# A fused transformer layer's expert stage: 192-row visits run four chunks of split products, then the raw products of the same four

## The chip, the cores and the metric

The kernel runs on one core of one Trainium2 chip. Its time is the time of one execution in microseconds; the median of several is given, and one more execution is profiled.

## The reference

One layer over 1024 latent tokens and 256 context tokens of width 1024, all float32: modulated RMSNorm, attention and a bidirectional mLSTM side by side, an output projection, and then a routed feed-forward with 32 experts, of which each token takes 4. The change touches the last part alone:

```python
def expert_block(args):
    xb, e = args
    gu = xb @ w_gu[e] + b_gu[e]
    glu = jnp.minimum(gu[:, :D_FF], SWIGLU_LIMIT)
    lin = jnp.clip(gu[:, D_FF:], -SWIGLU_LIMIT, SWIGLU_LIMIT)
    return (glu * jax.nn.sigmoid(SWIGLU_ALPHA * glu) * (lin + 1)) @ w_down[e] + b_down[e]
```

Here `w_gu[e]` is 1024 x 2048 and `w_down[e]` 1024 x 1024. The result of each row, times its gate and the modulation, is added to the token's row.

## The kernel before

The kernel is seven phases; the last, `phase_experts`, takes from about 905 us to the end. It goes over the experts in **visits**. A visit takes one expert and some of its rows; the experts are ordered by how many rows they have, and a visit's kind gives how many rows it takes. `MIXED` takes 192: a full part of 128 rows and a raw part of 64. `FULL` takes 128, `WIDE` 256 (two full parts), `NARROW` 64 and `LEAST` 32 (raw parts alone), `SPILL` 128. The order is six pairs of MIXED and FULL, two of MIXED and NARROW, three of WIDE and LEAST, three of WIDE and NARROW, then the spill visits. So there are eight MIXED visits.

**Weights.** An expert's weights are 12 chunks of 128 x 2048 (1 MB each), chunks 0 to 7 of `w_gu`, 8 to 11 of `w_down`, in 12 buffers `w[c]`. SP loads chunk c of the next visit when chunk c of this one is done with: for a visit behind a MIXED one when `s_used` has counted it (L2143, L2152), for the one behind a FULL visit when `s_lo` has (L2147). Chunks 0 to 3 make the first half of gate and up, 4 to 7 the second, 8 to 11 the result.

**Two kinds of product.** A full part uses split products. ACT copies a chunk to a high part `wh` (rounded, L2458, `s_hi`), DVE subtracts to get the low part `wl` (L2575, `s_lo`); there are three slots of each (`SLOTS`), chunk c has slot c % 3. PE multiplies high rows by high, high by low, low by high: 3 matmuls for each of 2 halves and 2 k-steps, 12 of 128 x 128 by 512 columns a chunk (L2312 for gate and up, L2326 for the result). A raw part uses the float32 chunk itself with a stationary operand of 64 columns, two column tiles side by side (L2307, L2321); the profile counts 8 such instructions a chunk.

**PE's order in a MIXED visit** (`visit` of the tensor block): for each chunk both parts, the full one first for even c, the raw one first for odd c. So raw products of two chunks stand together: full 0, raw 0, raw 1, full 1, full 2, raw 2, raw 3, full 3, and so on. The bias of the full part (L2297) opens the visit, that of the raw part (L2293) stands ahead of raw 0; both second ones stand ahead of chunk 4. Behind chunk 5 PE turns the first half of the hidden rows (L2283, six transposes), behind chunk 8 the second half, behind chunk 9 and behind chunk 10 the next visit's rows (L2272, four each); those behind chunks 8 and 10 thus stand between two raw products. `s_used` is raised once a chunk, by its last matmul.

**ACT** writes the high part of chunk c when `s_used` says that chunk c - 3 is done with (`split`, `this`, `ahead` for the next visit's first three), and between them the silus (L2470) and the high parts of turned rows. **DVE** writes the low parts, and when `s_used` says that four chunks are done it clamps gate and linear of both parts (`clamped`, L2593, L2598), multiplies them (`hidden`, L2607, `s_h`), takes the low parts of turned rows (L2568) and at the end the result (`result`, L2638, L2635). Each engine's order is written out by hand and is strict: what stands behind a wait waits with it. **POOL** gathers the rows of the visit after the next when PE has turned the next one's (`s_tp`) and scatters results.

Of the kernel before, what the change touches and what calls it, by code (L numbers as in the profile page):

```python
# [12 lines left out]
ALU = mybir.AluOpType  # L13
# [2036 lines left out]
def phase_experts(nc, a, m, PS):  # L2050
# [6 lines left out]
    with semaphores(nc, "experts") as sem:  # L2057
# [78 lines left out]
        with nc.Block() as block:  # L2136
# [127 lines left out]
            def _(pe):  # L2264
# [119 lines left out]
                with pe.Fori(0, N192) as i:  # L2384
                    visit(2 * i, 2 * i, MIXED, FOR_SMALL, 48 * i + 16)
                    visit(2 * i + 1, 2 * i + 1, FULL, FOR_BIG, 48 * i + 48)
                with pe.Fori(N192, NWIDE0) as i:
                    visit(2 * i, i + N192, MIXED, FOR_SMALL, 48 * i + 16)
                    visit(2 * i + 1, None, NARROW, FOR_BIG, 48 * i + 48)
# [40 lines left out]
            def _(act):  # L2430
# [47 lines left out]

                def visit(v, parts, before, following, banks, next_split, last=False):

                    def this(c):
                        split(c, v, v * NW + (c - SLOTS + 1))

                    def ahead(c):
                        if next_split:
# [32 lines left out]
                with act.Fori(0, N192) as i:  # L2518
                    visit(2 * i, MIXED, 6 * i, FULL, FOR_SMALL, True)
                    visit(2 * i + 1, FULL, 6 * i + 4, MIXED, FOR_BIG, True)  # L2520
                for i in range(N192, NWIDE0):
                    visit(2 * i, MIXED, 6 * i, None, None, False)
                    narrow(2 * i + 1, NARROW, 6 * i + 4, MIXED if i + 1 < NWIDE0 else WIDE)
# [33 lines left out]
            def _(dve):  # L2557
# [27 lines left out]

                def clamped(parts, j, v, before):

                    dve.wait_ge(s_used, v * NW + (4 * j + 4))
                    first = before + len(parts) * j
                    for p, part in enumerate(parts):  # L2590
                        b = part.second if j else part.first
                        n = H // part.tiles if part.tiles else H
                        dve.tensor_scalar(hid[p][:, 0:n], PS[:, b[0], 0:n], 7.0, ALPHA, ALU.min, ALU.mult).then_inc(s_g, 1)  # L2593
                    for p, part in enumerate(parts):
                        b = part.second if j else part.first
                        n = H // part.tiles if part.tiles else H
                        up = PS[:, b[0], n:2 * n] if part.tiles else PS[:, b[1], :]
                        dve.tensor_scalar(lin[p][:, 0:n], up, 7.0, -7.0, ALU.min, ALU.max).then_inc(s_cd, 1)  # L2598

# [41 lines left out]

                def visit(v, col, parts, before, n_split, n_eh, following, banks, next_split, last=False):

# [9 lines left out]
                    this(5)  # L2653
                    clamped(parts, 0, v, before)
                    this(6)
# [4 lines left out]
                    this(9)  # L2660
                    clamped(parts, 1, v, before)
                    hidden(parts, 1, before)
# [20 lines left out]
                def narrow(v, parts, col, before, n_split, n_eh, following=WIDE):  # L2683

                    tiles = parts[0].tiles

                    def keep_hidden(half, bank):
                        dve.wait_ge(s_tp, 4 * v + (3 + (2 * half if parts is LEAST else half)))
                        dve.tensor_scalar(hTr[0][:, 4 * half:4 * half + 4, 0:P // tiles], folded(bank, tiles), 1.0 / ALPHA, None, ALU.mult).then_inc(s_el, 1)
                    clamped(parts, 0, v, before)  # L2690
# [4 lines left out]
                    clamped(parts, 1, v, before)  # L2695
                    hidden(parts, 1, before)
                    keep_hidden(1, parts[0].upper)
                    split(0, n_split * NW + 1)
                    turn_kept(xT, 0, following, FOR_BIG[0], n_eh)
                    split(1, n_split * NW + 2)  # L2700
                    turn_kept(xT, 1, following, FOR_BIG[1], n_eh + 2)
                    result(parts, v)
                    split(2, n_split * NW + 3)
                with dve.Fori(0, N192) as i:
                    visit(2 * i, 3 * i, MIXED, 6 * i, 2 * i, 12 * i + 4, FULL, FOR_SMALL, True)
                    visit(2 * i + 1, 3 * i + 2, FULL, 6 * i + 4, 2 * i + 1, 12 * i + 10, MIXED, FOR_BIG, True)
                for i in range(N192, NWIDE0):
                    eh = 8 * i + 4 * N192
                    visit(2 * i, 3 * i, MIXED, 6 * i, i + N192, eh + 4, None, FOR_SMALL, False)
                    narrow(2 * i + 1, NARROW, 3 * i + 2, 6 * i + 4, i + (N192 + 1), eh + 8, MIXED if i + 1 < NWIDE0 else WIDE)  # L2710
# [142 lines left out]
```

## Time and profile before

| | |
|---|---|
| median of 3 runs | 2443.32 us (2442.1 to 2449.93) |
| the profiled execution | 2440.65 us, its span 2438.8 us |
| PE busy | 2330.0 us, 96% of the span |
| DVE, ACT busy | 1575.3 and 1078.0 us |
| mean granted TensorE clock | 0.979 of full speed |
| DMA | 556.74 MB, 228 GB/s over the span |

PE is TensorE's matmuls, PEld its weight loads, DVE VectorE, ACT ScalarE, POOL GpSimd, SP the engine that issues the loads. In a timeline, matmuls of one kind that follow one another are merged into one row with their count; a matmul's own duration is longer than the distance to the next, because they are pipelined, so runs are measured from start to start.

### The profile page before, as it was taken

How to read it: one execution, taken by the hardware profiler on the slowest of the kernel's cores; microseconds unless marked ns; L12 is line 12 of the kernel's file. 1: busy time of each engine (PE TensorE's matmuls, PEld its weight loads, DVE VectorE, ACT ScalarE, POOL GpSimd, SP SyncE). 2: the span in 40 equal slices, each digit the busy share in tenths (PEclk: the TensorE clock that was granted, in tenths of full speed). 3: DMA queues.
4: the chain of work that ended last, by engine and by line, in shares of the span. 5: the costliest groups of instructions: out<-in, count | busy, mean ns of one | idle time of the engine just before them, and what ended most of it. 6: DMA issues, size and time to landing. Idle time of an engine off the chain costs nothing.

```text
span 2438.8 us, 34440 instructions
## 1 busy us (share of the span) xinstructions
PE 2330.0 (96%) x12022; PEld 1612.1 (66%) x12022; DVE 1575.3 (65%) x1911; ACT 1078.0 (44%) x1392; POOL 526.1 (22%) x487
## 2 busy tenths in 40 slices
PE   5999988999998959999999999999999999999997
PEld 3997674555556746676766766557778768667775
DVE  3332756767656676876877867455556555549998
ACT  3332333444454234564655655324333323327776
POOL 0000041555676021111211211101100110102112
PEclk8999999999999969999999999999999999999999
DMA  8450031000013376987978979889789988979997
GB/s 300 156 179 23 19 106 75 8 4 7 1 55 106 123 260 221 326 281 265 338 252 295 322 248 316 295 315 367 270 302 379 318 299 306 332 247 386 382 386 259
DMA packets 241305, 556.74 MB, mean 228 GB/s; under 512 B 27841, under 2 KB 32354, under 8 KB 240098
## 3 DMA queue, kind: packets, MB, share of 16 engines
q1 hardware_dynamic: 225680, 509.49, 58.5%
q0 software_dynamic: 12704, 45.75, 7.0%
q8 instruction: 52, 0.85, 0.1%
q10 hardware_dynamic: 2834, 0.36, 0.1%
q14 instruction: 35, 0.29, 0.0%
HBM read 520.18 MB, written 34.96 MB: 228 GB/s over the span
## 4 chain that ended last, share of the span: by engine, by line
PE 57%; DMA 1%; DVE 1%; issue 1%; ACT 1%; POOL 1%; DVEq 0%; ACTq 0%; POOLq 0%
PE PS L2312 28%; PE PS L2326 13%; PE PS L2307 8%; PE PS L2321 4%; DMA acc_dram<-y,idxs 1%; PE PS L2272 1%; PE PS L2283 1%; PE PS L2297 1%; ACT wh L2458 1%; DVE wl L2575 0%; PE PS L2293 0%; POOL rt L2259 0%; DVE y L2638 0%; DVE hid L2593 0%; DVE hTl L2568 0%
## 5 line engine op out<-in xcount | busy, mean ns | idle before, releaser
L2575 DVE TENSOR_TENSOR wl<-w,wh 128x2048 fp32r<-128x2048 f32 x312 | 713.3, 2289 | 232.9 <-ACT wh L2458 231.7
L2458 ACT ACTIVATE wh<-w 128x2048 fp32r<-128x2048 f32 x312 | 597.7, 1916 | 393.5 <-PE PS L2312 265.1
L2312 PE MATMUL PS<-wh,xTh 128*128 128x512 f32 x1024 | 333.2, 407 | 0.0
L2312 PE MATMUL PS<-wl,xTh 128*128 128x512 f32 x1024 | 316.5, 390 | 0.0
L2312 PE MATMUL PS<-wh,xTl 128*128 128x512 f32 x1024 | 315.8, 390 | 0.0
L2204 POOL COPY idxg<-tokens 128x1 int32 (+1 forms) x47 | 28.5, 624 | 1023.9 <-PE PS L2272 950.6
L2312 PEld LDWEIGHTS PS<-wh,xTh 128*128 128x128 f32 x1024 | 187.9, 189 | 66.3 <-issue 28.1
L2312 PEld LDWEIGHTS PS<-wl,xTh 128*128 128x128 f32 x1024 | 192.5, 188 | 41.5
L2312 PEld LDWEIGHTS PS<-wh,xTl 128*128 128x128 f32 x1024 | 192.5, 188 | 40.9
L2307 PE MATMUL PS<-w,xTr 128*64 128x512 f32 (+1 forms) x1216 | 210.1, 527 | 0.0
L1118 POOL TENSOR_TENSOR acc<-acc,probT 128x512 f32<-128x512 f32 x128 | 174.2, 1361 | 24.8 <-ACT probT L1176 12.0
L2326 PE MATMUL PS<-wh,hTh 128*128 128x512 f32 x512 | 165.7, 405 | 2.3 <-DVE hTl L2568 2.3
L2326 PE MATMUL PS<-wl,hTh 128*128 128x512 f32 x512 | 158.9, 391 | 0.0
L2326 PE MATMUL PS<-wh,hTl 128*128 128x512 f32 x512 | 158.2, 390 | 0.0
L2219 POOL DMA_INDIRECT acc_dram<-y,idxs x47 | 109.1, 2322 | 188.7 <-DVE y L2638 121.4
L2470 ACT ACTIVATE hid<-hid 128x512 f32<-128x512 f32 (+2 forms) x96 | 49.5, 543 | 215.9 <-DVE hid L2593 215.9
L2307 PEld LDWEIGHTS PS<-w,xTr 128*64 128x64 f32 (+1 forms) x1216 | 67.4, 128 | 113.2 <-issue 103.4
L1248 DVE TENSOR_REDUCE negmax<-PS 128x1 f32<-128x1280 f32 x64 | 95.5, 1492 | 56.4 <-PE PS L1377 55.7
L1176 ACT ACTIVATE probT<-PS 128x512 f32<-128x512 f32 x160 | 93.0, 597 | 87.7 <-PE PS L1399 81.2
L2326 PEld LDWEIGHTS PS<-wh,hTh 128*128 128x128 f32 x512 | 90.2, 188 | 32.0 <-issue 13.0
L2321 PE MATMUL PS<-w,hTr 128*64 128x512 f32 (+1 forms) x608 | 110.9, 532 | 0.0
L2326 PEld LDWEIGHTS PS<-wh,hTl 128*128 128x128 f32 x512 | 96.1, 188 | 21.3
(443 smaller groups left out, 3474.7 us busy)
## 6 DMA issues: line engine op xcount, KB each, us to landing
w<-in_w_gu_dram SPq DMA_DIRECT2D x544, 512.0 KB, 11.3
w<-in_w_down_dram SPq DMA_DIRECT2D x136, 1024.0 KB, 12.5
later_wmod<-in_w_mod_dram SPq DMA_DIRECT2D x8, 2048.0 KB, 8.0
wmod<-in_w_mod_dram SPq DMA_DIRECT2D x8, 1024.0 KB, 14.5
x<-in_x_dram SPq DMA_DIRECT2D x8, 512.0 KB, 7.8
rowm<-rowm_dram SPq DMA_DIRECT2D x16, 256.0 KB, 3.3
w_out<-in_w_out_dram SPq DMA_DIRECT2D x1, 4096.0 KB, 12.6
ox<-in_x_dram SPq DMA_DIRECT2D x8, 512.0 KB, 4.3
```

The lines of the kernel that those rows point to most:

```text
L1118: pool.tensor_tensor(acc[half][:, :], acc[half][:, :], probT[:, op + 1, :], ALU.add).then_inc(s_acc, 1)
L1176: act.activation(probT[:, n % NT, :], PS[:, T0 + n % 3, :], ACT.Exp).then_inc(s_ex, 1)
L1248: dve.tensor_reduce(negmax[:, u:u + 1], flat[:, 0:KEYS], AX.X, ALU.max, negate=True).then_inc(s_mx, 1)
L2204: pool.tensor_copy(idxg[p][:, :], m.tokens[:, bass.ds(col + p, 1)]).then_inc(s_pc, 1)
L2219: pool.indirect_dma_start(out=a["acc"], out_offset=bass.IndirectOffsetOnAxis(ap=idxs[p][0:n, 0:1], axis=0), in_=y[p][0:n, :], in_offset=No ...
L2307: mm = pe.matmul(PS[tile_rows(part, u), b[0], 0:2 * n], xTr[part.n][:, k, 0:P // part.tiles], wrv[c][:, kk, :, n * u:n * u + n], start=Fal ...
L2312: mm = pe.matmul(PS[:, b[g], :], x[part.n][:, k, :], ws[s][:, kk, g, :], start=False, stop=end and x is xTl)
L2321: mm = pe.matmul(PS[tile_rows(part, u), b[0], 0:D // part.tiles], hTr[part.n][:, k, 0:P // part.tiles], wdn[c][:, kk, tile_cols(part, u)], ...
L2326: mm = pe.matmul(PS[:, b[g], :], x[part.n][:, k, :], ws[s][:, kk, g, :], start=begin and x is hTh and ws is whv, stop=end and x is hTl)
L2458: act.activation(wh[c % SLOTS][:, :], w[c][:, :], ACT.Copy).then_inc(s_hi, 1)
L2470: act.activation(hid[p][:, 0:n], hid[p][:, 0:n], ACT.Silu).then_inc(s_sg, 1)
L2575: dve.tensor_tensor(wl[c % SLOTS][:, :], w[c][:, :], wh[c % SLOTS][:, :].bitcast(F32), ALU.subtract).then_inc(s_lo, 1)
```

## The change

A MIXED visit on PE gets a function of its own, `mixed`. In each of three quarters it runs the split products of four chunks and then the raw products of the same four. Each split chunk raises a new semaphore, `s_parts`; `s_used` is raised by the raw product of each chunk. All transposes now stand behind split products; the raw part's biases stand at the beginning of the raw run. ACT's high parts of MIXED visits, and the next visit's first three behind one, wait for `s_parts` in place of `s_used`. DVE clamps the full part on `s_parts` and the raw part on `s_used`, one behind the other. The helpers `gate_clamped` and `linear_clamped` are the old bodies of `clamped`.

```diff
+        s_parts = sem("chunk_parts_used_by_mixed")
...
+                def mixed(v, i, split, rows_in):
+                    full, raw = MIXED
+                    pe.wait_ge(s_sel, v + 1)
+                    for quarter in range(3):
+                        chunks = range(4 * quarter, 4 * quarter + 4)
+                        product = down if quarter == 2 else gate_up
+                        if quarter == 0:
+                            pe.wait_ge(s_el, 4 * v + 1)
+                            bias(full, 0)
+                        for c in chunks:
+                            pe.wait_ge(s_lo, split * NW + (c + 1))
+                            if c == 4:
+                                pe.wait_ge(s_y, v + 1)
+                                bias(full, 1)
+                            if c == 8:
+                                pe.wait_ge(s_el, 4 * v + 3)
+                            if c == 10:
+                                pe.wait_ge(s_el, 4 * v + 4)
+                            for kk in range(2):
+                                mm = product(full, c, kk)
+                            mm.then_inc(s_parts, 1)
+                            if c == 5:
+                                pe.wait_ge(s_h, 2 * v + 1)
+                                turn_hidden(MIXED, 0)
+                            if c == 8:
+                                pe.wait_ge(s_h, 2 * v + 2)
+                                turn_hidden(MIXED, 1)
+                            if c == 9:
+                                pe.wait_ge(s_xg, rows_in)
+                                turn_rows(FOR_SMALL, 0)
+                            if c == 10:
+                                turn_rows(FOR_SMALL, 1)
+                        if quarter == 0:
+                            pe.wait_ge(s_el, 4 * v + 2)
+                            bias(raw, 0)
+                        if quarter == 1:
+                            bias(raw, 1).then_inc(s_bias, 1)
+                        for c in chunks:
+                            for kk in range(2):
+                                mm = product(raw, c, kk)
+                            mm.then_inc(s_used, 1)
...
-                    visit(2 * i, 2 * i, MIXED, FOR_SMALL, 48 * i + 16)
+                    mixed(2 * i, i, 2 * i, 48 * i + 16)
...
-                def split(c, v, used):
+                def split(c, v, used, by=s_used):
...
-                        act.wait_ge(s_used, used)
+                        act.wait_ge(by, used)
...
+                        if parts is MIXED:
+                            split(c, v, nth * NW + (c - SLOTS + 1), s_parts)
...
+                        if next_split and parts is MIXED:
+                            split(c, v + 1, nth * NW + (NW + c - SLOTS + 1), s_parts)
...
+                    if parts is MIXED:
+                        dve.wait_ge(s_parts, nth * NW + (4 * j + 4))
+                        gate_clamped(0, parts[0], j)
+                        linear_clamped(0, parts[0], j)
+                        dve.wait_ge(s_used, v * NW + (4 * j + 4))
+                        gate_clamped(1, parts[1], j)
+                        linear_clamped(1, parts[1], j)
+                        return
```

## Rows read from the trace of the kernel before

**Rows 1.** The page: PE's busy time, and DVE's costliest group

```profile
PE 2330.0 (96%) x12022; PEld 1612.1 (66%) x12022; DVE 1575.3 (65%) x1911; ACT 1078.0 (44%) x1392; POOL 526.1 (22%) x487
...
L2575 DVE TENSOR_TENSOR wl<-w,wh 128x2048 fp32r<-128x2048 f32 x312 | 713.3, 2289 | 232.9 <-ACT wh L2458 231.7
```

**Rows 2.** PE's longest waits, 905 to 2390 us: us, times, longest one

```profile
PE PS L2297 <- DVE xTl L2568: 6.3, 5, 2.2
```

**Rows 3.** By stretch: length, busy PE, PEld, DVE, ACT, POOL; clock, DMA share, GB/s

```profile
1006.70:1066.70 60.00, 60.00 (x270) 35.14 (x269) 39.83 (x34) 27.21 (x23) 8.67 (x7) 1.00 0.75 254
1066.70:1103.20 36.50, 36.50 (x173) 29.65 (x172) 33.97 (x27) 26.56 (x20) 7.75 (x7) 1.00 1.00 351
...
1549.50:1573.80 24.30, 24.30 (x122) 8.80 (x122) 11.11 (x17) 7.09 (x9) 4.72 (x3) 1.00 1.02 334
```

**Rows 4.** Timeline of PE, one MIXED visit: start, us, instructions

```profile
1006.68 0.61 PE L2297 MATMUL PS<-bias,sel 96*128 96x512 bf16 x2
...
1009.96 0.41 PE L2293 MATMUL PS<-bias,sel 96*64 96x512 bf16 x2
...
1013.73 0.73 PE L2312 MATMUL PS<-wh,xTh 128*128 128x512 f32 x2
...
1016.59 0.62 PE L2312 MATMUL PS<-wh,xTh 128*128 128x512 f32 x2
...
1019.40 3.65 PE L2307 MATMUL PS<-w,xTr 128*64 128x512 f32 x16
1022.98 0.73 PE L2312 MATMUL PS<-wh,xTh 128*128 128x512 f32 x2
...
1025.84 0.61 PE L2297 MATMUL PS<-bias,sel 96*128 96x512 bf16 x2
...
1026.71 0.73 PE L2312 MATMUL PS<-wh,xTh 128*128 128x512 f32 x2
...
1036.09 0.82 PE L2283 MATMUL PS<-ident,hid 128*128 128x128 f32 x6
...
1039.57 3.65 PE L2307 MATMUL PS<-w,xTr 128*64 128x512 f32 x16
...
1048.82 1.94 PE L2321 MATMUL PS<-w,hTr 128*64 128x512 f32 x8
1050.69 0.88 PE L2283 MATMUL PS<-ident,hid 128*128 128x128 f32 x6
...
1053.36 0.73 PE L2326 MATMUL PS<-wh,hTh 128*128 128x512 f32 x2
...
1066.69 0.61 PE L2297 MATMUL PS<-bias,sel 96*128 96x512 bf16 x2
```

**Rows 5.** Timeline of PE, in a FULL and in a NARROW visit

```profile
1067.60 0.62 PE L2312 MATMUL PS<-wl,xTh 128*128 128x512 f32 x2
...
1072.59 0.61 PE L2312 MATMUL PS<-wh,xTh 128*128 128x512 f32 x2
...
1549.77 7.04 PE L2307 MATMUL PS<-w,xTr 128*64 128x512 f32 x32
1556.63 0.38 PE L2293 MATMUL PS<-bias,sel 96*64 96x512 bf16 x2
...
1573.77 0.61 PE L2297 MATMUL PS<-bias,sel 96*128 96x512 bf16 x2
...
1574.69 0.62 PE L2312 MATMUL PS<-wl,xTh 128*128 128x512 f32 x2
```

**Rows 6.** Timeline of DVE, second half of MIXED, then first of NARROW

```profile
1046.21 1.02 DVE L2593 TENSOR_SCALAR hid<-PS 128x512 f32<-128x512 f32 x2 [0.41 <-PE PS L2312]
...
1048.74 1.03 DVE L2607 SCALAR_TENSOR_TENSOR hid<-lin,hid 128x512 f32<-128x512 f32 x2 [0.58 <-ACT hid L2470]
...
1556.85 0.43 DVE L2593 TENSOR_SCALAR hid<-PS 128x256 f32<-128x256 f32 x1 [4.51 <-PE PS L2307]
...
1557.84 0.43 DVE L2607 SCALAR_TENSOR_TENSOR hid<-lin,hid 128x256 f32<-128x256 f32 x1 [0.23 <-ACT hid L2470]
```

More of the change, by code:

```diff
@@ L2384, in _ @@
                 with pe.Fori(0, N192) as i:
-                    visit(2 * i, 2 * i, MIXED, FOR_SMALL, 48 * i + 16)
+                    mixed(2 * i, i, 2 * i, 48 * i + 16)
                     visit(2 * i + 1, 2 * i + 1, FULL, FOR_BIG, 48 * i + 48)
                 with pe.Fori(N192, NWIDE0) as i:
-                    visit(2 * i, i + N192, MIXED, FOR_SMALL, 48 * i + 16)
+                    mixed(2 * i, i, i + N192, 48 * i + 16)
                     visit(2 * i + 1, None, NARROW, FOR_BIG, 48 * i + 48)
@@ L2477, in bias_parts, with visit @@
                     act.activation(gparts[:, :, :], graw[:, :, :], ACT.Copy).then_inc(s_gk, 1)
-                def visit(v, parts, before, following, banks, next_split, last=False):
+                def visit(v, parts, before, following, banks, next_split, last=False, nth=None):
                     def this(c):
-                        split(c, v, v * NW + (c - SLOTS + 1))
+                        if parts is MIXED:
+                            split(c, v, nth * NW + (c - SLOTS + 1), s_parts)
+                        else:
+                            split(c, v, v * NW + (c - SLOTS + 1))
                     def ahead(c):
-                        if next_split:
+                        if next_split and parts is MIXED:
+                            split(c, v + 1, nth * NW + (NW + c - SLOTS + 1), s_parts)
+                        elif next_split:
                             split(c, v + 1, v * NW + (NW + c - SLOTS + 1))
@@ L2584, in _, with gate_clamped, linear_clamped, clamped @@
                 dve.wait_ge(s_gb, 16)
-                def clamped(parts, j, v, before):
+                def gate_clamped(p, part, j):
+                    n = H // part.tiles if part.tiles else H
+                    bank = (part.second if j else part.first)[0]
+                    dve.tensor_scalar(hid[p][:, 0:n], PS[:, bank, 0:n], 7.0, ALPHA, ALU.min, ALU.mult).then_inc(s_g, 1)
+                def linear_clamped(p, part, j):
+                    b = part.second if j else part.first
+                    n = H // part.tiles if part.tiles else H
+                    up = PS[:, b[0], n:2 * n] if part.tiles else PS[:, b[1], :]
+                    dve.tensor_scalar(lin[p][:, 0:n], up, 7.0, -7.0, ALU.min, ALU.max).then_inc(s_cd, 1)
+                def clamped(parts, j, v, before, nth):
+                    if parts is MIXED:
[6 more added lines that the diff above has]
+                        return
                     dve.wait_ge(s_used, v * NW + (4 * j + 4))
-                    first = before + len(parts) * j
                     for p, part in enumerate(parts):
-                        b = part.second if j else part.first
-                        n = H // part.tiles if part.tiles else H
-                        dve.tensor_scalar(hid[p][:, 0:n], PS[:, b[0], 0:n], 7.0, ALPHA, ALU.min, ALU.mult).then_inc(s_g, 1)
+                        gate_clamped(p, part, j)
                     for p, part in enumerate(parts):
[L2595 to L2598, printed above, removed]
+                        linear_clamped(p, part, j)
                 def hidden(parts, j, before):
@@ L2640, in result, with visit @@
                     ins.then_inc(s_y, 1)
-                def visit(v, col, parts, before, n_split, n_eh, following, banks, next_split, last=False):
+                def visit(v, col, parts, before, n_split, n_eh, following, banks, next_split, last=False, nth=None):
                     def this(c):
@@ L2653, in visit @@
                     this(5)
-                    clamped(parts, 0, v, before)
+                    clamped(parts, 0, v, before, nth)
                     this(6)
@@ L2660, in visit @@
                     this(9)
-                    clamped(parts, 1, v, before)
+                    clamped(parts, 1, v, before, nth)
                     hidden(parts, 1, before)
@@ L2689, in keep_hidden @@
                         dve.tensor_scalar(hTr[0][:, 4 * half:4 * half + 4, 0:P // tiles], folded(bank, tiles), 1.0 / ALPHA, None, ALU.mult).then_inc(s_el, 1)
-                    clamped(parts, 0, v, before)
+                    clamped(parts, 0, v, before, None)
                     hidden(parts, 0, before)
@@ L2694, in narrow @@
                     keep_hidden(0, parts[0].lower)
-                    clamped(parts, 1, v, before)
+                    clamped(parts, 1, v, before, None)
                     hidden(parts, 1, before)
@@ L2704, in _ @@
                 with dve.Fori(0, N192) as i:
-                    visit(2 * i, 3 * i, MIXED, 6 * i, 2 * i, 12 * i + 4, FULL, FOR_SMALL, True)
+                    visit(2 * i, 3 * i, MIXED, 6 * i, 2 * i, 12 * i + 4, FULL, FOR_SMALL, True, nth=i)
                     visit(2 * i + 1, 3 * i + 2, FULL, 6 * i + 4, 2 * i + 1, 12 * i + 10, MIXED, FOR_BIG, True)
```

6 lines of the change are left out of this document (3 added, 3 removed).

## The prediction

> **What bounds the kernel now.** The page first: PE is busy for 2330.0 of the 2438.8 us span [rows 1]. What matters is the expert stage, from 905 to 2390 us, and there the longest entry in the list of PE's waits is 6.3 us, in five waits [rows 2]. The busy time by stretch shows a 192-row visit and the 128-row visit behind it: PE is busy for all 60.00 and all 36.50 us, at a granted clock of 1.00, that is at 2.4 GHz; DVE has 39.83 and 33.97 us of work in them [rows 3]. So PE sets the time in every mixed visit, and only what shortens PE's own stream, or makes it wait, can move the end. The timeline of PE shows one such visit as runs of split products (L2312, L2326) and of raw products (L2307, L2321); it lasts from 1006.68 to 1066.69, 60.01 us [rows 4]. There are 8 of them (6 before full visits, 2 before narrow ones).
>
> **No product is removed.** Two pitches come from runs without a turn in them. Split matmuls: from 1067.60 to 1072.59 eleven pairs start, 4.99 us, 0.2268 each, so a chunk of 12 takes 2.72 us [rows 5]. Raw: the narrow visit's 32 matmuls, four chunks, start at 1549.77 and the next thing at 1556.63, so a chunk takes 1.715 us [rows 5]. A mixed visit needs 12 of each: 32.7 + 20.6 = 53.2 us. The other 6.8 us are biases, transposes and turns between the two kinds of run, and of these the change takes a part.
>
> **Turns.** From 1013.73 to 1022.98 PE does two split chunks and two raw ones and is back at the same point: 9.25 us for 2 x 2.72 + 2 x 1.715 = 8.87 us [rows 4]. A turn there and back costs 0.38 us. Its parts: the first split chunk takes 2.86 us (entry 0.14), the second 2.81 (leaving 0.09), the raw pair 3.58 instead of 3.43 (0.15). Before, the raw chunks go in pairs (0 with 1, 2 with 3, and so on), six raw runs a visit; after, there are three runs of four chunks. Three turns fewer: 3 x 0.38 = 1.14 us.
>
> **Transposes that leave the raw run.** The six hidden transposes behind chunk 8 stand inside a raw pair: from 1048.82 to 1053.36 is 4.54 us, against 3.58 for a raw pair alone, so they cost 0.96. The same six behind chunk 5 stand between split chunks: from 1036.09 to 1039.57 they and a split chunk take 3.48 us, less 2.81 for the chunk: 0.67 [rows 4]. After the change all stand between split chunks: 0.29 us less. The four row transposes behind chunk 10 move in the same way; what goes is the second entry and leaving of a raw run around them, not their own time, so I cost them the same, 0.29 (bounds 0 and 0.29).
>
> **Biases.** At chunk 4 the full part's bias and the raw part's bias stand between two split chunks: 1025.84 to 1026.71, 0.87 us, and an entry of 0.14: 1.01. After, the full bias stands ahead of a split run, which costs 0.47 (1006.68 to 1009.96 is 3.28, less 2.72 and 0.09), and the raw bias stands at a turn, which costs 0.19 (1009.96 to 1013.73 is 3.77, against 3.58) [rows 4]. That is 0.35 us less. And two of the three remaining returns to split work begin with a bias (chunk 4, the next visit's chunk 0): the bias then takes the place of the first split matmul, and the entry of 0.14 is gone, twice, 0.28 us. The trace shows raw, bias, split at the end of a narrow visit: from the bias at 1573.77 to the third split matmul at 1574.69 is 0.92 us, and behind split products, from 1066.69 to 1067.60, it is 0.91 [rows 4, 5]. A raw run of four chunks between two split runs is not in the trace; I price it by the pitch of 1.715 and one entry and leaving.
>
> **The sum.** 1.14 + 0.29 + 0.29 + 0.35 + 0.28 = 2.35 us a visit, and 8 visits give 18.8 us. Without the row transposes' 0.29 it would be 2.06 and 16.5 us. The profiled execution takes 2440.65 us, so it would take 2421.9; it lies 2.7 us under the median of the runs, 2443.32, and the forecast for the median is 2424.5 us.
>
> **Where something could come late.** Three things are rearranged for it.
> Hidden halves: DVE now clamps the full part when the split run ends, far ahead, and the raw part when the raw run ends. What PE then has before the hidden transposes is two split chunks and a bias at chunk 5 (0.26 + 5.7 us) and only chunk 8 at the second half (2.72 + 0.14 = 2.86 us, where before it was 1046.21 less 0.2 to 1050.69, 4.7 us). The path at the second half, priced from the narrow visit: raw run ends, DVE starts 0.22 later, and the raw product of gate and linear is done at 1558.27, 1.42 after 1556.85, with the silu within it [rows 5, 6]. The full part's product goes in ahead of the raw one: a pair takes 1.03 and the narrow one 0.43, so 0.6 more. The half is ready 0.22 + 1.42 + 0.6 = 2.2 us after the raw run, at the most, against 2.86: 0.6 us to spare. At chunk 5 a low part of 2.29 us (L2575 [rows 1]) lies in between: 4.5 against about 6.0. Queued behind DVE's new wait are the products, the gate columns, the selector and the low parts of chunks 6 and 10; the tightest of these, chunk 10, has chunk 9 and two groups of transposes of cover more than the half has. ACT's silu of the raw part waits for the same clamp.
> High and low parts: slots of the high part come free at the split product, and in a run of four split chunks ACT and DVE must deliver one per 2.72 us. The 128-row visit has just this pace, and PE is busy for 36.50 of 36.50 us in it [rows 3]. In the raw runs nothing is asked for, so they catch up; the added wait of ACT costs nothing there.
> Weight loads: SP issues the load of chunk c for the next visit when the raw product of c is done. Chunk 0's raw product now stands behind four split chunks instead of one, so its load goes out 8 us later, and that of chunk 8 some 11 us later (its raw run of two ended 16.0 us before the visit's end, at 1050.69; now it is done 5.2 before); SP stands behind each, the later loads with it. POOL's next gather, which waits for the row transposes, starts some 7 us earlier, out of the way of the last four loads. By the DMA's rate under (c) these loads have landed some 7 us into the visit behind, which asks for its chunk 8 over 14 us after its start, so I cost it at nothing. If loads were late, every microsecond would be PE's.
>
> The added signals are 12 increments a visit at the ends of split chunks. In the 128-row visit each chunk ends with one as well, and the 0.2268 pitch runs on through it [rows 5], so their price is nothing. The Trainium skill, page "TensorE: Matmul & The Clock Gate", section "The cost: per-tile semaphore tail", puts 26.3 ns on each increment; as an estimate from that page 96 of them would be 2.5 us and the time 2427.0. The trace speaks against it here, because the pitch has no room for it.
>
> **Rivals.** (a) The hidden half comes late. The whole path took 3.56 us before (1046.21 to 1049.77 [rows 6], with a high part in ACT's way); if it stays so long behind the raw run, PE waits 3.56 + 0.2 - 2.86 = 0.9 us a visit, 7.2 in all, and the time is 2431.7. For it: the margin is thin. Against: most of that path is the full part's, which is now done earlier. (b) The change doesn't do what it says: the 0.38 us goes with the chunks and not with the turns, as a loss that each raw chunk pays once its rows and weights alternate with split ones, and longer runs pay it all the same. Then nothing is gained: 2443. Against: the narrow visit's run of 32 shows no such loss. The Trainium skill, page "TensorEngine Tiling (Array Packing)", section "Key Properties", says that a change of tiling mode drains TensorE, which would be a price for each turn; it names no size, so the sum has none of it, and it is one reason why (b) has no more than 0.07. (c) Slower: the weights. In the last 5.2 us of a mixed visit four loads of 1.05 MB are freed, and the full visit's twelve follow; with gathers and scatters (an estimate: 320 rows of 4 KB in, as many out and added, some 3 MB) that is 19.8 MB. At the 351 GB/s of that stage [rows 3] they are in after 56 us, 15 us into the next mixed visit, with chunk 3 some 24 us earlier in the queue. PE asks for chunk 3 8.4 us into it, and the high and the low part need some 4.2 of them (2.29 for the low one [rows 1], somewhat less for the high one), so it must land by 4.2. It lands 9 us before the visit begins. If the bunched loads ran slower, chunk 3 would be late below 250 GB/s; at 210 GB/s it would be 8 us late in each of 8 visits, 64 - 19 = 45 us slower, 2488, and from about 230 down it is slower by what can be measured. For it: the DMA share is 1.00 in the full visit and 1.02 in the narrow one, and loads that were spread over the mixed visit now come in three bunches. Against: 351 and 334 GB/s were moved at just that share [rows 3]. In the two narrow pairs the margin is smaller (chunk 0 must land 20 us after the mixed visit's end, 24.3 less 4.2, and 8.2 MB, itself and some 3 MB of rows among them, have 25 us, 328 GB/s), but two visits a few microseconds late take back a part of the gain only; the range has them. (d) The clock: raw runs of 7 us might lower it. The narrow visit is nothing but raw runs, and the granted clock is 1.00 in it [rows 3], so I give this no chance.
>
> **How the numbers follow.** Forecast 0.81, (a) 0.08, (b) 0.07, (c) 0.04. Under 0.3% (7.3 us) two measurements of this kernel can't be told apart. Forecast and (a) are faster by more: 0.89; (b) is the same: 0.07; (c) is slower: 0.04. The range takes in the forecast with its bounds (savings of 16 to 19 us, and 3 us of difference between medians) and (a): 2420 to 2433.
>
> **What would show it.** In the profile after, a mixed visit lasts 57.7 us (57.5 to 58.2), with runs of 48, 24, 24 and three times 12 split matmuls and three runs of 32 raw ones; the raw runs take about 7.0 us each. The full and narrow visits keep 36.5 and 24.3 us, the wide ones stay as they are. PE's waits stay as short as they are; a new row of PE waiting for DVE's hidden product would be (a), PE or ACT waiting for a landing (c). The prediction is wrong if the visits keep 60 us with PE busy, or if PE idles ahead of chunk 3, chunk 9 or the hidden transposes.

## The result, and the profile after

| | before | after |
|---|---|---|
| median | 2444.82 us of 6 runs (2442.1 to 2451.38) | 2429.95 us of 6 runs (2425.31 to 2432.9) |
| ratio | | 0.9935, 95% interval 0.9924 to 0.9947 |
| profiled execution, its span | 2440.65, 2438.8 us | 2429.25, 2427.4 us |
| the 8 mixed visits, sum | 481.78 us | 463.98 us |
| of these, the five between two full visits, each | 60.01 us | 57.84 to 57.91 us |
| a full visit, a narrow visit | 36.5, 24.25 us | 36.5, 24.23 us |
| the three pairs of WIDE and LEAST and the three of WIDE and NARROW, sum | 537.35 us | 544.82 us |

The kernel became faster by 14.9 us in the medians (15.9 by the ratio, 13 to 19 by its interval), against 18.8 forecast; 2429.95 lies in the range of 2420 to 2433. The profiled executions differ by 11.4 us only, and the stretches say why: the mixed visits give 17.8 us, the pairs with wide visits, which the diff doesn't touch, take 7.5 back, all of it in the three wide visits behind LEAST ones. Of the 1.1 us that are left, 0.7 lie ahead of the first mixed visit (908.61 us before, 907.87 after).

One run below was a slow one, 3929.9 us at a granted clock of 0.556: one of the twelve of before with the rows moved, whose figures here leave it out.

The page of after, engines first. PE's busy time fell by 14.2 us, its idle time rose by 2.8 (108.8 to 111.6):

```profile
span 2427.4 us, 34446 instructions
PE 2315.8 (95%) x12022; PEld 1620.4 (67%) x12022; DVE 1571.3 (65%) x1911; ACT 1082.2 (45%) x1392; POOL 533.0 (22%) x487
```

The timeline of PE in one mixed visit of after (start, us, instructions), the one that answers to [rows 4]:

```profile
1003.63 0.60 PE L2298 MATMUL PS<-bias,sel 96*128 96x512 bf16 x2
...
1009.54 0.74 PE L2313 MATMUL PS<-wh,xTh 128*128 128x512 f32 x2
1010.12 0.63 PE L2313 MATMUL PS<-wl,xTh 128*128 128x512 f32 x2
...
1015.24 0.41 PE L2294 MATMUL PS<-bias,sel 96*64 96x512 bf16 x2
1015.48 7.03 PE L2308 MATMUL PS<-w,xTr 128*64 128x512 f32 x32
1022.45 0.60 PE L2298 MATMUL PS<-bias,sel 96*128 96x512 bf16 x2
...
1034.80 7.03 PE L2308 MATMUL PS<-w,xTr 128*64 128x512 f32 x32
1041.76 0.73 PE L2327 MATMUL PS<-wh,hTh 128*128 128x512 f32 x2
...
1044.62 0.82 PE L2284 MATMUL PS<-ident,hid 128*128 128x128 f32 x6
...
1054.52 7.09 PE L2322 MATMUL PS<-w,hTr 128*64 128x512 f32 x32
1061.54 0.61 PE L2298 MATMUL PS<-bias,sel 96*128 96x512 bf16 x2
```

Three raw runs of 32 matmuls, each 6.96 to 7.02 us from start to start, stand where six of 16 were; from the first bias to the last it is 57.91 us. The windows of that visit, of the full one behind it and of a narrow one answer to [rows 3] (length, then busy PE, PEld, DVE, ACT, POOL, granted clock, DMA share, GB/s):

```profile
1003.60:1061.50 57.90, 57.90 (x269) 35.84 (x268) 39.37 (x34) 29.68 (x24) 11.29 (x9) 1.00 0.71 250
1061.50:1098.10 36.60, 36.60 (x175) 29.70 (x174) 33.86 (x26) 24.66 (x19) 6.61 (x4) 1.00 1.04 371
1533.40:1557.60 24.20, 24.20 (x122) 8.85 (x118) 11.06 (x17) 7.17 (x9) 4.69 (x3) 1.00 1.03 355
```

PE is still busy all of the time, at 2.4 GHz, long raw runs included, and the bunched loads move at 371 and 355 GB/s. What changed elsewhere is in the list of PE's waits (us, times, longest one), which answers to [rows 2]:

```profile
PE PS L2298 <- DVE xTl L2617: 10.6, 7, 2.5
PE PS L2327 <- DVE hTl L2617: 1.6, 5, 0.3
```

The first line is a bias that waits for DVE's low part of turned rows: 10.6 us against 6.3. One of the seven waits opens the first visit, 2.2 us before and 2.1 after; the others stand at wide visits behind LEAST ones, three of them, 1.05 us each, ahead of the visit in both kernels. So two questions stand: are the 2.35 us a visit made of the steps that were summed, and do the 7.5 us in the wide visits come from the change?

### The profile page after: what moved, and what is told of

Read it like the earlier page. It is cut to its first block, busy times and chain, and to the rows that moved or that the text cites. A ratio compares the mean times of both kernels' runs of the same rounds, so it can differ in the third digit from the quotient of the medians.

```text
span 2427.4 us, 34446 instructions
## 1 busy us (share of the span) xinstructions
PE 2315.8 (95%) x12022; PEld 1620.4 (67%) x12022; DVE 1571.3 (65%) x1911; ACT 1082.2 (45%) x1392; POOL 533.0 (22%) x487
## 4 chain that ended last, share of the span: by engine, by line
PE 57%; DVE 2%; DMA 2%; issue 1%; ACT 1%; POOL 0%; DVEq 0%; ACTq 0%; POOLq 0%
PE PS L2313 28%; PE PS L2327 13%; PE PS L2308 7%; PE PS L2322 4%; DMA acc_dram<-y,idxs 2%; PE PS L2273 1%; PE PS L2284 1%; PE PS L2298 1%; ACT wh L2502 1%; DVE wl L2624 0%; PE PS L2294 0%; DVE y L2700 0%; DVE outs L2815 0%; DVE xTl L2617 0%; DVE rows L2811 0%
## 5 line engine op out<-in xcount | busy, mean ns | idle before, releaser
L2205 POOL COPY idxg<-tokens 128x1 int32 (+1 forms) x47 | 36.3, 790 | 971.7 <-PE PS L2273 897.8
L2638 DVE TENSOR_SCALAR hid<-PS 128x512 f32<-128x512 f32 (+2 forms) x96 | 55.6, 590 | 120.9 <-PE PS L2308 106.2
L2327 PEld LDWEIGHTS PS<-wl,hTh 128*128 128x128 f32 x512 | 96.1, 188 | 21.1
## 6 DMA issues: line engine op xcount, KB each, us to landing
wmod<-in_w_mod_dram SPq DMA_DIRECT2D x8, 1024.0 KB, 14.2
```

The costliest lines, as they stand in the source:

```text
L2327: mm = pe.matmul(PS[:, b[g], :], x[part.n][:, k, :], ws[s][:, kk, g, :], start=begin and x is hTh and ws is whv, stop=end and x is hTl)
L2638: dve.tensor_scalar(hid[p][:, 0:n], PS[:, bank, 0:n], 7.0, ALPHA, ALU.min, ALU.mult).then_inc(s_g, 1)
```

## Experiments on the mixed visit

**The same kernel once more,** to see which stretches repeat.

> The changed kernel once more, unchanged. In its profiled execution the eight 192-row visits took 57.6 to 57.9 us each (the first 59.24) against 60.0 to 60.1 before, 17.9 us less in all with the visits between them, but the three wide visits behind a 32-row visit took 73.60, 71.17 and 74.22 us against 71.12, 70.21 and 70.21, 7.5 us more. Theory A (chance): these three waits on landing weights, and the falls of the granted clock behind two of them, come and go between executions of either kernel; then the 192-row visits repeat to 0.1 us here and the three wide visits come out differently, and the ratio to before is 0.992 to 0.994. Theory B (caused by the change): the three wide visits take 71 to 74 us again, 4 us or more above before's in sum, and the gain stays at 11 to 16 us.

Measured: median 2428.54 us of 6 runs, ratio 0.9931 (0.9915 to 0.9947). The mixed visits sum to 464.07 us, 0.09 from the first profile. The three wide visits behind LEAST ones took 77.19, 73.93 and 70.19 us, against 73.60, 71.17 and 74.22 in the first profile of the same program. A mixed visit's length belongs to the kernel; that of a wide visit behind a LEAST one to the execution.

**Groups of two and of one.** PE's `mixed` with its chunks in groups of two (six raw runs, as before the change) or of one (twelve), transposes and biases where the change has them.

```diff
-                    for quarter in range(3):
-                        chunks = range(4 * quarter, 4 * quarter + 4)
-                        product = down if quarter == 2 else gate_up
+                    for group in range(NW // 2):
+                        chunks = range(2 * group, 2 * group + 2)
+                        product = down if chunks[0] >= 8 else gate_up
```

> Groups of two chunks in place of four: split 0, 1, raw 0, 1, split 2, 3, raw 2, 3 and so on, all else as in the changed kernel, so six raw runs a visit as before the change, but the transposes stand between split products and the biases at the turns. Theory of turns (0.38 us for a raw run's entry and leaving): a 192-row visit takes 57.85 + 3 x 0.38 = 59.0 us, somewhat less where the short split runs take away the wait at chunk 2 (some 0.1). Rival, the price goes with the chunks: 57.85 us, since no chunk is added or removed. A second rival, that all of the gain is the transposes and biases: 57.85 too.

> Groups of one chunk: twelve raw runs a visit. If each raw run costs 0.38 us, nine more than in the changed kernel: 57.85 + 3.4 = 61.3 us a visit, 1.2 us slower than before the change, and as 6 more turns than with groups of two 2.3 us above that kernel's visit. If the price goes with the chunks: 57.85. Whole kernel by the turns: some 27 us slower than the changed kernel, 8 visits x 3.4.

Measured: groups of two 2437.1 us (7 runs, ratio 0.9962, 0.9947 to 0.9976), mixed visits of 58.76 us; groups of one 2452.32 us in one run, mixed visits of 61.22 us (those between two full visits, here and below; 57.87 is their mean in after). The time goes with the turns, so rival (b) falls: the raw chunks are the same twelve in all three kernels. From twelve raw runs to six it is 2.46 us, 0.41 a turn; from six to three 58.76 - 57.87 = 0.89, 0.30 a turn. The sum had 0.38. The timeline of PE in the kernel with groups of one shows a single turn there and back:

```profile
1014.87 1.94 PE L2308 MATMUL PS<-w,xTr 128*64 128x512 f32 x8
1016.74 0.74 PE L2313 MATMUL PS<-wh,xTh 128*128 128x512 f32 x2
...
1019.73 1.94 PE L2308 MATMUL PS<-w,xTr 128*64 128x512 f32 x8
1021.59 0.74 PE L2313 MATMUL PS<-wh,xTh 128*128 128x512 f32 x2
```

From 1016.74 to 1021.59 is 4.85 us for a split chunk and a raw one, 2.72 + 1.715 without a turn, so the turn costs 0.41.

Before the change there were six raw runs too, so before against groups of two is everything but the turns: 60.01 - 58.76 = 1.25 us. The terms for hidden transposes, row transposes, biases and entries were 0.29 + 0.29 + 0.35 + 0.28 = 1.21; the last paragraph of this section parts them by place.

**PE's old order with the new signals.** Both semaphores are raised and waited for as in the changed kernel, but PE goes through the chunks as before; DVE's result waits for `s_parts` as well, since the last split product now comes last.

```diff
                     mm = down(part, c, kk) if c >= 8 else gate_up(part, c, kk)
+                    if both:
+                        mm.then_inc(s_used if part.tiles else s_parts, 1)
...
-                    mixed(2 * i, i, 2 * i, 48 * i + 16)
+                    visit(2 * i, 2 * i, MIXED, FOR_SMALL, 48 * i + 16, both=True)
```

> The order of the products on PE as before the change, but with the change's signals and waits: split products raise the new semaphore, high parts wait for it, DVE clamps the full part on it and the raw part on the old one, and the result waits for both. It tells the order apart from the waits. If the gain is the order's alone: 60.0 us a visit, as before. If the 12 more increments cost what the page on TensorE says, 26.3 ns each: 60.3. If the earlier high parts bring something by themselves: below 60.0.

Measured: 2452.41 us in one run; the mixed visits take 60.01 us, to the hundredth as in [rows 4], and all eight sum to 481.75 against 481.78. The 12 increments a visit, and the waits of ACT and DVE that go with them, cost PE nothing; the whole gain of a mixed visit is PE's order. By the 26.3 ns of the Trainium skill, page "TensorE: Matmul & The Clock Gate", section "The cost: per-tile semaphore tail", the visit would as an estimate have been 60.33 us. That page has the figure as part of the tail behind matmuls in concurrent tiles; in this dense stream of matmuls the measurement shows none of it. The run's total is no better than before although nothing in its mixed visits is worse: its three wide visits took 74.08, 72.76 and 76.19 us, the worst set of all, with PE's order of before. That speaks against PE's new order as the cause of the 7.5 us; the new signals are still in this kernel.

**A late hidden half on purpose.** DVE takes chunk 10's low part before the hidden product in the second half.

```diff
                     clamped(parts, 1, v, before, nth)
+                    if parts is MIXED:
+                        this(10)
                     hidden(parts, 1, before)
```

> The changed kernel, but in the second half of a 192-row visit DVE takes chunk 10's low part (2.28 us) before the product of gate and linear. In the changed kernel's trace the hidden half was ready 1.05 us before PE turned it (1043.57 against 1044.62). If that margin is the whole cover, PE waits 2.28 - 1.05 = 1.2 us at that place in each visit: 59.1 us a visit, 10 us slower than the changed kernel in all. If PE has more cover than the trace shows: 57.85. If the delay also holds up chunk 10 and 11: more than 59.1.

Measured: 2436.6 us in one run. The mixed visits took 59.10 to 59.13 us, some 1.25 more than after, and PE has the wait that rival (a) described. DVE in one visit, then PE in the same visit, then the new row in PE's waits:

```profile
1046.43 2.28 DVE L2624 TENSOR_TENSOR wl<-w,wh 128x2048 fp32r<-128x2048 f32 x1
1048.63 1.02 DVE L2669 SCALAR_TENSOR_TENSOR hid<-lin,hid 128x512 f32<-128x512 f32 x2
```

```profile
1049.71 0.88 PE L2284 MATMUL PS<-ident,hid 128*128 128x128 f32 x6 [1.05 <-DVE hid L2669]
```

```profile
PE PS L2284 <- DVE hid L2669: 8.4, 8, 1.1
```

In the changed kernel itself the second half is ready in time:

```profile
1041.88 0.42 DVE L2638 TENSOR_SCALAR hid<-PS 128x256 f32<-128x256 f32 x1 [4.29 <-PE PS L2308]
...
1042.55 1.02 DVE L2669 SCALAR_TENSOR_TENSOR hid<-lin,hid 128x512 f32<-128x512 f32 x2
```

It ends at 1043.57, and PE turns the half at 1044.62: 1.05 us to spare. A delay of 2.28 less 1.05 is 1.23, which is what the visit lost. So the margin is real, rival (a) did not happen, and it would have been paid in full had the path been longer.

**Chunk 2's low part.** One thing in the changed visit's timeline was not in the sum: the split pair at 1009.54, where chunk 2 begins, has 0.58 us to the next pair and not 0.45, and it follows split products. DVE there, behind a full visit:

```profile
1003.80 2.29 DVE L2624 TENSOR_TENSOR wl<-w,wh 128x2048 fp32r<-128x2048 f32 x1 [0.65 <-ACT wh L2502]
1006.01 1.27 DVE L2700 SCALAR_TENSOR_TENSOR y<-PS,gcol,g2bc 128x1024 f32<-128x1024 f32 x1
1007.20 6.77 DVE L2624 TENSOR_TENSOR wl<-w,wh 128x2048 fp32r<-128x2048 f32 x3
```

The full visit's result stands ahead of chunk 2's low part, which is done only some 2.29 us after 1007.20, at 1009.49, 0.05 before its product starts. The experiment puts the low part first.

```diff
+                    if parts is FULL:
+                        ahead(2)
                     result(parts, v)
-                    ahead(2)
+                    if parts is not FULL:
+                        ahead(2)
```

> The changed kernel, but at the end of a 128-row visit before a 192-row one DVE takes chunk 2's low part before the visit's result, not behind it. In the changed kernel's trace that low part is ready at 1009.48 and PE's chunk 2 begins at 1009.54 with one matmul 0.11 us too long and ten somewhat slow, and the first run of 48 takes 11.29 to 11.36 us, but 11.19 in the visit behind a narrow one. If this low part is the cause: 11.19 in all visits behind full ones, 57.7 us a visit; the whole kernel by some 0.8 us. If it is not: 11.3 as it was. Chunk 3's low part could come late in its place: more than 11.3.

Measured: 2428.76 us in one run; mixed visits 57.73 us, 0.14 less, while the one behind a narrow visit keeps its 57.64; the one at the same place reaches the raw part's bias 11.44 us after its first bias (1003.25 to 1014.69), where after took 11.61 (1003.63 to 1015.24). PE where chunk 2 begins (at 1009.16) in this kernel:

```profile
1009.16 0.62 PE L2313 MATMUL PS<-wh,xTh 128*128 128x512 f32 x2
1009.61 0.61 PE L2313 MATMUL PS<-wl,xTh 128*128 128x512 f32 x2
```

The pair has its 0.45 us again. In the eight visits it is 0.67 us (463.31 against 463.98), which totals can't show.

**Where in the visit the terms lie.** Two marks cut a visit into thirds, the full part's second bias (chunk 4) and the first product of chunk 8. In the kernel before the first mark stands in [rows 4], the second is this row:

```profile
1046.01 0.62 PE L2326 MATMUL PS<-wh,hTh 128*128 128x512 f32 x2
```

The same marks in the kernel with groups of two, and in the one with chunk 2's low part first:

```profile
1004.93 0.61 PE L2298 MATMUL PS<-bias,sel 96*128 96x512 bf16 x2
...
1023.95 0.61 PE L2298 MATMUL PS<-bias,sel 96*128 96x512 bf16 x2
...
1043.61 0.73 PE L2327 MATMUL PS<-wh,hTh 128*128 128x512 f32 x2
...
1063.69 0.60 PE L2298 MATMUL PS<-bias,sel 96*128 96x512 bf16 x2
```

```profile
1003.25 0.61 PE L2298 MATMUL PS<-bias,sel 96*128 96x512 bf16 x2
...
1021.89 0.60 PE L2298 MATMUL PS<-bias,sel 96*128 96x512 bf16 x2
...
1041.21 0.73 PE L2327 MATMUL PS<-wh,hTh 128*128 128x512 f32 x2
...
1060.99 0.60 PE L2298 MATMUL PS<-bias,sel 96*128 96x512 bf16 x2
```

| us | first third | second | last |
|---|---|---|---|
| before | 19.16 | 20.17 | 20.68 |
| groups of two | 19.02 | 19.66 | 20.08 |
| low part first | 18.64 | 19.32 | 19.78 |
| after | 18.82 | 19.31 | 19.78 |

From groups of two to groups of four one turn goes in each third: 0.38 us where nothing stood at it, 0.34 where six hidden transposes stood at it, 0.30 where four row transposes did. Before against groups of two is 0.65 us in the first two thirds, where the forecast's biases and entries lie (0.35 + 0.28; in the last third either kernel has two returns to bare split products), and 0.60 in the last, where the moved transposes are (0.58). After differs from the kernel with the low part first in the first third alone.

## Experiments on the wide visits

A wide visit's second bias waits for DVE's low part of the second half of its turned rows. Behind a LEAST visit, ACT and DVE take that half only behind chunk 1's high and low part, and chunk 1 has then to have landed. ACT at the first wide visit, before and after (the bracket is ACT's idle time and what ended it):

```profile
1741.31 1.91 ACT L2458 ACTIVATE wh<-w 128x2048 fp32r<-128x2048 f32 x1 [1.61 <-DMA w<-in_w_gu_dram]
1743.13 1.07 ACT L2441 ACTIVATE xTh<-PS 128x512 fp32r<-128x512 f32 x2
```

```profile
1723.50 1.92 ACT L2502 ACTIVATE wh<-w 128x2048 fp32r<-128x2048 f32 x1 [2.44 <-DMA w<-in_w_gu_dram]
1725.32 1.06 ACT L2485 ACTIVATE xTh<-PS 128x512 fp32r<-128x512 f32 x2
```

and PE there, in after:

```profile
1723.83 0.61 PE L2298 MATMUL PS<-bias,sel 96*128 96x512 bf16 x2 [1.05 <-DVE xTl L2617]
...
1728.99 0.60 PE L2298 MATMUL PS<-bias,sel 96*128 96x512 bf16 x2 [1.81 <-DVE xTl L2617]
...
1730.38 1.06 PE L2313 MATMUL PS<-wh,xTl 128*128 128x512 f32 x2
1731.24 1.06 PE L2313 MATMUL PS<-wh,xTh 128*128 128x512 f32 x2
```

Relative to the visit's start ACT begins chunk 1 at -1.16 us before and at -0.33 after. The length follows it, over all executions profiled in which ACT and DVE have this order behind a LEAST visit:

| kernel | start of chunk 1's high part, three visits (us) | length (us) |
|---|---|---|
| before | -1.16, -2.86, -2.71 | 71.12, 70.21, 70.21 |
| after | -0.33, -1.13, 0.32 | 73.60, 71.17, 74.22 |
| after once more | 2.37, -0.01, -2.88 | 77.19, 73.93, 70.19 |
| groups of two | -0.33, 1.57, 0.41 | 73.56, 75.34, 72.69 |
| groups of one | 0.59, -1.62, -2.89 | 74.50, 70.66, 70.21 |
| old order | 0.14, 0.45, 1.14 | 74.08, 72.76, 76.19 |
| late hidden half | -1.17, -2.89, -0.12 | 71.13, 70.21, 72.16 |
| low part first | -0.07, 0.13, -0.30 | 72.24, 74.02, 73.61 |

Where visits of nearly the same start differ (72.24 and 74.02), the clock does it. PE's wait is only half of what the first wide visit in after lost. The windows (columns as above) of the first wide visit in after, and of 3.4 us within it:

```profile
1723.80:1797.40 73.60, 71.76 (x320) 58.23 (x320) 39.20 (x38) 25.77 (x21) 7.13 (x10) 0.98 0.91 331
...
1730.30:1733.70 3.40, 3.40 (x9) 2.69 (x9) 2.78 (x2) 0.86 (x1) 2.23 (x2) 0.50 1.06 392
```

Of 73.60 us, 1.84 are idle, and behind the wait the granted clock is 0.50, the level of 1.2 GHz, for 3.4 us; that is where the pairs above take 0.85 us instead of 0.45, and it costs about 1.6 us more (84 split matmuls take 20.88 us there, and 19.23 at the full clock in the same visit of before). Chunk 0 can land late as well, and then the LEAST visit ahead is the longer one: 15.25 us with groups of two, 15.34 and 15.42 in the old order, 14.97 with both edits, against 14.35.

**The second half of the rows ahead of chunk 1.** In the LEAST visit alone, ACT and DVE take the turned rows of both halves first; then chunk 1's landing has a whole chunk of PE's work as cover. The edit goes on the kernel before and on the one after, so their difference is the change without these waits. ACT's part (DVE's is the same):

```diff
-                    split(1, v + 1, None)
+                    if parts is not LEAST:
+                        split(1, v + 1, None)
                     rows_kept(1, following, FOR_BIG[1], 4 * v + 6)
+                    if parts is LEAST:
+                        split(1, v + 1, None)
```

> The kernel before, with one edit outside the change: behind a 32-row visit ACT and DVE take the second half of the next visit's turned rows before they split that visit's chunk 1, and not behind it. Then PE's wait for those rows, 1.3 to 2.9 us behind the wide visit's chunk 0, no longer hangs on the landing of chunk 1. Theory A (the wide visits behind 32-row visits vary by chance with that landing, in both kernels): the three take 70.0 to 70.3 us each in place of 71.1, 70.2, 70.2, the clock doesn't fall in them, the median is 2438 to 2441 us instead of 2445 to 2446, and the runs lie closer together than 9 us. Theory B (before has no such loss, the change made it): the median stays at 2445 and the spread too.

> The changed kernel with the same edit behind 32-row visits. Theory A: the three wide visits take 70.0 to 70.3 us instead of 71 to 77, and the median is 2419 to 2422 us, 17.5 to 18.5 us under the kernel before with the same edit, which is the gain of the 192-row visits alone. Theory B: the difference between the two edited kernels stays at 12 to 16 us.

Measured, on the same chip beside the same runs of before (2446.59 us): before with the edit 2438.8 us, ratio 0.9968 (0.9957 to 0.9979); after with the edit 2420.0, ratio 0.9900 (0.9885 to 0.9916). All three wide visits took 69.98 us (69.99 in the first kernel), and the granted clock is 1.00 in all of them. (Before's own profile, 2440.65 us, was one of its fast executions and had lost little there, so the edit takes only 2.5 us off its span, 2436.3 against 2438.8, but 7.8 off the median; the runs lie between 2436.7 and 2440.4 us, and those of before beside them between 2440.3 and 2452.6.) In the second, ACT and then PE at the first of them:

```profile
1724.43 1.92 ACT L2502 ACTIVATE wh<-w 128x2048 fp32r<-128x2048 f32 x1 [2.51 <-DMA w<-in_w_gu_dram]
```

```profile
1723.70 0.61 PE L2298 MATMUL PS<-bias,sel 96*128 96x512 bf16 x2 [1.05 <-DVE xTl L2620]
...
1726.87 0.60 PE L2298 MATMUL PS<-bias,sel 96*128 96x512 bf16 x2
```

Chunk 1 begins at 0.73, later than in 21 of the 24 visits of the table, and the second bias, at 1726.87, waits for nothing. So the dependency is what turned a late landing into time. Between the two kernels lie 18.8 us in medians, 16.6 by the ratios and 18.1 in spans, 17.6 of them in the mixed visits: 481.80 against 464.20. The totals can't part these; what the stretches show for the change itself is the 17.6, and the forecast was 18.8.

**Both edits on the changed kernel,** `rows_kept` first and chunk 2's low part first.

> The changed kernel with both edits: rows ahead of chunk 1's split behind 32-row visits, and chunk 2's low part ahead of the result at the end of the 128-row visits before 192-row ones. Each has shown its effect in the trace (the three wide visits 69.98 us each; the 192-row visits 57.73 instead of 57.88). If they add up: 192-row visits of 57.73 and 57.64 us, wide visits of 69.98 to 70.0, a span of 2417.5 us and a median of 2418.5 to 2420, 27 us under the kernel before. If the later result of the 128-row visits holds something up: their followers or the scatters come late, and the median is above 2420.

Measured: 2419.53 us (6 runs, 2417.78 to 2422.45), ratio 0.9892 (0.9872 to 0.9911), mixed visits of 57.73 to 57.74 us. This version beats both kernels, by 27.3 us against before as measured beside it (2446.83); that it beats the one with the first edit alone (2420.0) can't be told from these runs.

## Why the prediction was right, and where it was not

- **What bounds the visit.** Right: PE is busy 57.90 of 57.90 us after, and each microsecond taken from its order came off the visit. Chunk pitches, full visits (36.5) and narrow ones (24.23) stayed.
- **The terms of the sum.** Forecast 2.35 us a visit; measured 60.01 - 57.87 = 2.14 between full visits, 2.35 and 2.46 in the two ahead of narrow ones (raw products now meet raw products at their end, and the second has no full visit ahead of it), 2.29 in the first; in the eight together 17.8 instead of 18.8. The moved transposes, biases and saved entries together are 1.25 for a forecast 1.21, and by thirds 0.65 and 0.60 for 0.63 and 0.58. The three turns were to give 1.14 and gave 0.89 in after, 58.76 - 57.73 = 1.03 once chunk 2's delay was out of the way. The last 0.11 is in the second and last third: transposes stand at the turn there in groups of two, and taking that turn away brings 0.34 and 0.30 us, while the bare one brings the 0.38 of the sum.
- **The step that failed** is the one on high and low parts, "The 128-row visit has just this pace" and the conclusion that nothing is lost by it. The pace is the same, the start is not: a full visit stands behind a mixed one, a mixed one behind a full visit whose result, 1.27 us of DVE, lies ahead of chunk 2's low part. In the old order raw products stood between chunks 0 and 2 and covered it; in a run of four split chunks nothing does. Measured 0.14 us in each visit behind a full one.
- **"The wide ones stay as they are", "PE's waits stay as short as they are".** Missed: 10.6 us of waits against 6.3, and 7.5 us in the stretch. The prediction saw the 6.3 us in [rows 2] and took them for a fixed cost, where they were the outcome of one execution. The cause is the landing of chunk 1 behind a LEAST visit. It doesn't take the change: the same program gave other lengths the second time, PE's old order gave longer ones, before itself has 7.8 us of its median from it, and with the dependency moved both kernels have 69.98 or 69.99 us. Whether the change makes such landings somewhat more frequent isn't shown: the edit took 8.5 to 10 us off the changed kernel's medians (2428.54 and 2429.95) against 7.8 off before's. The first comparison of medians, 14.9 against 18.8, fits with that; but its interval reaches to 19 us, so a loss isn't proved by totals.
- **The number.** The forecast of 2424.5 was missed by 5.4 us: 3.9 in the difference, and 1.5 because before's median over six runs is 2444.82 and not 2443.32. That 2429.95 is in the range is in part luck: the wide visits weren't in it, and its upper end was there for rival (a), which did not come.
- **Rival (a), the late hidden half.** It did not come: 1.05 us to spare where 0.6 was forecast as the least. Made late on purpose, it cost the delay less the margin, as the rival's working had it (1.25 for 1.23 us).
- **Rival (b), no gain from fewer turns.** Refuted by 61.22, 58.76 and 57.87 us for twelve, six and three raw runs. The Trainium skill, page "TensorEngine Tiling (Array Packing)", section "Key Properties", has a change of tiling mode drain TensorE. The runs agree that each change has a price, and give it a size here, 0.30 to 0.41 us there and back; that a drain is what takes it they don't show.
- **Rival (c), late weights.** Refuted: 371 and 355 GB/s in the full and the narrow visit against 351 and 334 before [rows 3], far from the 230 to 250 where it would have decided, and no wait of PE for a high or low part in the mixed visits.
- **Rival (d), the clock.** In the mixed visits it stayed at 1.00, as given, but for the first, which begins at 0.50 in both kernels (from 909 to 911 us). It did fall, in wide visits and behind PE's waits, where no rival had put it.
- **Signals.** At nothing, and nothing they cost: 60.01 with and without.

Open: what makes chunk 1 land some 3 us earlier or later in one execution than in another (0.32 and -2.88 at the third wide visit of the changed kernel), and what the first mixed visit's 2.29 us (61.53 to 59.24) are made of: it has no full visit ahead of it, so chunk 2's delay of 0.14 isn't in it, but it begins at the low clock, and it took 59.24 to 59.37 us in the five executions with groups of four and an early hidden half.

## What to carry to other kernels

On a TensorE that is never idle, price an order by its turns: count the changes between full-array and column-tiled matmuls, and where biases and transposes stand, since transposes inside a column-tiled run pay a second entry and leaving. When a run of the demanding kind gets longer, check the start of it and not only its pace: what the feeding engines still have to do from the visit before now lies bare. And when two profiles differ in a stretch that the edit doesn't touch, compare the kernel with itself first; here a strict order that put a DMA's landing ahead of rows that were already there cost some 8 us, beside a change worth 17 to 19.

## What the runs showed of the hardware

A turn between 128-column matmuls and pairs of 64-column ones costs 0.38 us there and back between runs of two chunks, 0.41 between runs of one, and only 0.34 or 0.30 where transposes stand at it. At short waits of PE the granted clock fell to 0.50 for 3.4 or 6.8 us: in after behind waits of 1.81 and 2.46 us, in the second run of it at 4.54 (6.8 us) and 2.14. It doesn't go by the wait's length alone: waits of 2.04 us (late hidden half, third wide visit) and 2.10 (low part first, the first) left it at 1.00, and so did one of 2.60 us in the old order's second wide visit, with 2.03 ahead of the visit, as this window shows beside the third's, with a wait of 3.29:

```profile
1830.40:1903.20 72.80, 70.20 (x324) 57.09 (x328) 39.19 (x38) 26.08 (x21) 8.16 (x10) 1.00 0.90 333
1918.50:1994.70 76.20, 72.86 (x320) 58.92 (x320) 39.19 (x38) 26.07 (x21) 8.83 (x10) 0.96 0.87 318
```

That is 70.20 busy us against 72.86 for the same matmuls. So a wait of some 2 us could cost its length or nearly twice that: in one execution (low part first) a wait of 2.10 gave a visit of 72.24 us and one of 1.87 a visit of 73.61, where 69.98 is the length without. And the landing of one 1 MB chunk, taken against PE's own progress, lay in one execution of a kernel more than 2 us into the visit and in another before its start.
